# Splitting the inputs of four projections in quarters, each next to the weight pieces that need it

## The chip, the cores and the metric

The kernel runs on one core of a Trainium2 chip. The metric is device time in microseconds (us) for one execution, median of several. A core has TensorE (PE: matmuls, and PEld: its weight loads), VectorE (DVE), ScalarE (ACT), GpSimd (POOL), and queues of DMA transfers, most of them issued by SyncE (SP). Each engine works through its own program in order and waits on semaphores that others raise.

## The reference

Two transformer blocks over 256 tokens with 2048 features, in float32. Cut to what matters:

```python
# first block
u = rmsnorm(h, mix_norm_w)
p = u @ w_in                          # columns for DeltaNet, then for RWKV
h = h + concat([o_dn, o_rw]) @ w_out  # mixer output
h = h + memory_cross_attention(...)
h = h + square(relu(rmsnorm(h, ffn_norm_w) @ w1)) @ w2   # MLP, 2048 -> 8192 -> 2048
x = rmsnorm(h, final_norm_w)
# second block; c is one vector
mod = silu(c) @ w_mod + b_mod + mod_layer      # six vectors: shift, scale, gate
h = rms_norm(x, norm1_g) * (1 + scale1) + shift1
proj = h @ w_in_2                     # second mixer, 2560 columns
x = x + gate1 * (y @ w_out_2)
x = x + gate2 * hierarchical_moe(...) # 32 experts, 2 per token
```

## The kernel before

The stages follow each other in blocks (`nc.Block`): at a block's end all engines meet, and at its start each takes up its next program. On the way from one to the next some 0.3 us pass.

**Split products.** The large matmuls keep float32 accuracy with TensorE's fast format (`fp32r`): a matrix a is split into a high part, which is a copy in that format made by ScalarE, and a low part, a minus its high part, made by VectorE. The product is then three matmuls: high x high, low x high and high x low. Both factors are split, the weights piece by piece as TensorE goes, and the input once at the start of the stage. The input is 128 x 16 chunks x 256 tokens, that is 4096 elements per partition.

The change touches four stages that do so:

- `rwkv_project` (class `SplitTiles`, methods L284 to L325). 24 output tiles; each is one product over 16 chunks, in two halves of 8 chunks. A weight piece is a half tile, 128x1024, with one buffer per half. TensorE spends 24 matmuls of 256 columns on a half. The first piece of the product reads only chunks 0 to 7 of the input.
- `mixer_out` (class `SplitRows`, L350 to L395): output 256 x 2048 in 4 groups of 512 columns. A group is 8 pieces of 2 chunks each, 128x1024, in 4 buffers; TensorE spends 12 matmuls of 512 columns on one. Piece p reads chunks 2p and 2p+1 of the input.
- `mlp` (L2067, class `Ffn`): 16 blocks of 512 hidden features. `order` lists the pieces (128x2048, 3 high and 3 low buffers, 4 raw ones that DMA fills): four up pieces of block 0, then in turn four up pieces of a block and four down pieces of the one before. An up piece covers 4 chunks of the input and takes 48 matmuls of 256 columns. VectorE also sums the modulation here (`sum_after`, L603): from piece 4 on, 96 multiply-adds over 128x2048, whose weights arrive in `mod_raw` beside the MLP's.
- `second_mixer` (L2242 on): `SplitRows` with 5 groups.

**Order at a stage's start.** In the first, second and fourth of these ScalarE makes the whole high part in two halves (`input_high`), then the high parts of weight pieces; VectorE makes both low halves (`input_low`), then low parts of pieces. TensorE waits for the low part of its first piece. In `mlp` each engine makes the input's part in one instruction, in a block of its own, ScalarE also calculates silu(c) there, and the pieces start in the next block. The buffer `shared`, which holds the MLP's input u, is the one in which the modulation is summed: GpSimd clears it (`mod.clear`, L597), SP then loads the bias into it (`loads_with`, with weight load 6), and VectorE adds from there. `deltanet_project` uses `SplitTiles` too and keeps its order.

Of the kernel before, what the change touches and what calls it, by code (L numbers as in the profile page):

```python
# [10 lines left out]
F32 = mybir.dt.float32  # L11
# [252 lines left out]
class SplitTiles:  # L264
# [62 lines left out]
class SplitRows:  # L327
# [22 lines left out]
    def input_high(self, act, x):  # L350
        for n in range(2):
            act.activation(self.x_hi[:, 8 * n:8 * n + 8], x[:, 8 * n:8 * n + 8, :], ACT.Copy).then_inc(self.k.act_sem, 1)

    def input_low(self, dve, x):
        for n in range(2):
            dve.wait_ge(self.k.act_sem, self.k.act_n + n + 1)
            dve.tensor_tensor(self.x_lo[:, 8 * n:8 * n + 8], x[:, 8 * n:8 * n + 8, :],
                              self.x_hi[:, 8 * n:8 * n + 8].bitcast(F32), ALU.subtract)
# [448 lines left out]
def deltanet_project(nc, k, tiles, qkvz, dn):  # L807
# [3 lines left out]
    with nc.Block(no_gpsimd_drain=True) as block:  # L811
# [324 lines left out]
def rwkv_project(nc, k, tiles, u, mix):  # L1136
# [5 lines left out]
    with nc.Block(no_gpsimd_drain=True) as block:  # L1142
# [24 lines left out]
        @block.scalar  # L1167
        def _(act):
            tiles.input_high(act, u)
            with act.Fori(0, 3) as i:  # L1170
                for m in range(8):
                    tiles.high(act, m, (0, 1), turn=i)

        @block.vector
        def _(dve):
            s.eng = dve

            tiles.input_low(dve, u)
# [8 lines left out]
            tiles.low(dve, 0, (0, 1))  # L1187
# [22 lines left out]
    k.act_n += 2  # L1210
# [2250 lines left out]
```

## Time and profile before

| what | us |
|---|---|
| median of 3 runs | 2546.53 |
| lowest, highest | 2545.34, 2548.73 |
| the profiled execution | 2547.53 |
| its span, first to last instruction | 2545.9 |
| busy in it: TensorE, VectorE, ScalarE | 2268.4, 1335.5, 789.8 |
| mean granted TensorE clock, share of full speed | 0.922 |

All times in the rows are from the start of the span of that one execution. A row of the timeline has the start, the duration, engine, source line, and what is written from what; a row with xN stands for N instructions of a kind in a row, with the time from the start of the first to the end of the last. In square brackets is how long the engine had been idle, and who released it. The names are the kernel's tensors: `rw_u_hi` and `rw_w_lo` are the input's high and the weight's low part in RWKV, `out_` in the mixer output, `in_` in the second mixer, `u_` and `ffn_w_` in the MLP.

### The profile page before, as it was taken

Reading aid. Unit: us, or ns where it says so; the run is one execution under the profiler, and the core shown is the slowest. Engines: PE = TensorE matmul, PEld = TensorE weight load, DVE = VectorE, ACT = ScalarE, POOL = GpSimd, SP = SyncE. Lnnn points to the kernel's source line nnn. Section 1 sums busy time; section 2 is a strip of 40 time slices with the busy share of each in tenths; the row PEclk is TensorE's granted clock in tenths of the full one; section 3 lists DMA queues with packets and bytes.
Section 4 is the critical chain, followed back from the end, with each engine's and each line's share of the span. In section 5 each row is a group of like instructions: output and inputs, shape, how many; then the busy total and the mean of one; then the engine's idle time right before and its main releaser. Section 6 shows DMA issues by size and latency. Waiting matters only on the chain. (4 is left out here: it accounts for less than half of the span.)

```text
span 2545.9 us, 40044 instructions
## 1 busy us (share of the span) xinstructions
PE 2268.4 (89%) x17032; PEld 1829.4 (72%) x17032; DVE 1335.5 (52%) x1604; ACT 789.8 (31%) x917; POOL 18.6 (1%) x62
## 2 busy tenths in 40 slices
PE   7998799878889987999999999997979787888884
PEld 7998799677867657899999899985854443444441
DVE  4776655565453125888787988865552411111112
ACT  4444333311243024434343434335430211111110
POOL 0000000000000000000000000000000000000000
PEclk8999899877889998999999999998989788889987
DMA  5453035100044316888798888845420599999998
GB/s 207 180 198 133 2 132 198 58 2 1 2 184 179 133 59 250 334 332 321 283 356 321 323 323 325 341 152 205 187 98 33 233 419 426 427 423 427 422 428 330
DMA packets 67288, 597.51 MB, mean 235 GB/s; under 512 B 9518, under 2 KB 9774, under 8 KB 16686
## 3 DMA queue, kind: packets, MB, share of 16 engines
q1 hardware_dynamic: 56906, 572.15, 56.2%
q10 hardware_dynamic: 9216, 12.60, 1.4%
q0 software_dynamic: 1008, 10.49, 1.0%
q8 instruction: 121, 1.98, 0.3%
q14 instruction: 37, 0.30, 0.0%
HBM read 674.88 MB, written 14.68 MB: 271 GB/s over the span
## 5 line engine op out<-in xcount | busy, mean ns | idle before, releaser
L2052 ACT ACTIVATE ffn_w_hi<-ffn_raw 128x2048 fp32r<-128x2048 f32 x128 | 245.0, 1916 | 372.0 <-PE psum L2097 368.7
L2059 DVE TENSOR_TENSOR ffn_w_lo<-ffn_raw,ffn_w_hi 128x2048 fp32r<-128x2048 f32 x128 | 292.6, 2289 | 90.7 <-ACT ffn_w_hi L2052 90.7
L2095 PE MATMUL psum<-u_hi,ffn_w_hi 128*128 128x256 f32 x1024 | 293.9, 287 | 15.0 <-DVE ffn_w_lo L2059 13.9
L2096 PE MATMUL psum<-u_lo,ffn_w_hi 128*128 128x256 f32 x1024 | 293.3, 286 | 0.0
L2097 PE MATMUL psum<-u_hi,ffn_w_lo 128*128 128x256 f32 x1024 | 293.3, 286 | 0.0
L2921 PE MATMUL psum<-moe_raw,moe_x_t 128*32 128x512 f32 x1536 | 217.8, 700 | 70.5 <-DMA moe_raw<-in_moe 62.9
L614 DVE SCALAR_TENSOR_TENSOR shared<-mod_raw,c_silu,shared 128x2048 f32<-128x2048 f32 x96 | 225.3, 2347 | 0.0
L2095 PEld LDWEIGHTS psum<-u_hi,ffn_w_hi 128*128 128x128 f32 x1024 | 200.2, 196 | 15.8 <-DVE ffn_w_lo L2059 14.1
L2096 PEld LDWEIGHTS psum<-u_lo,ffn_w_hi 128*128 128x128 f32 x1024 | 200.0, 195 | 0.4
L2097 PEld LDWEIGHTS psum<-u_hi,ffn_w_lo 128*128 128x128 f32 x1024 | 200.1, 195 | 0.0
L2096 PE MATMUL psum<-ffn_w_lo,ffn_hid_hi 128*128 128x512 f32 x512 | 199.4, 389 | 0.0
L2095 PE MATMUL psum<-ffn_w_hi,ffn_hid_hi 128*128 128x512 f32 x512 | 199.4, 389 | 0.0
L2097 PE MATMUL psum<-ffn_w_hi,ffn_hid_lo 128*128 128x512 f32 x512 | 199.3, 389 | 0.0
L2921 PEld LDWEIGHTS psum<-moe_raw,moe_x_t 128*32 128x32 f32 x1536 | 49.2, 120 | 179.1 <-issue 151.0
L321 PE MATMUL psum<-dn_u_hi,dn_w_hi 128*128 128x256 f32 x512 | 146.4, 286 | 0.0
L323 PE MATMUL psum<-dn_u_hi,dn_w_lo 128*128 128x256 f32 x512 | 145.6, 284 | 0.0
L322 PE MATMUL psum<-dn_u_lo,dn_w_hi 128*128 128x256 f32 x512 | 145.6, 284 | 0.0
L3066 DVE TENSOR_TENSOR moe_hid<-moe_silu,psum 128x64 f32<-128x64 f32 x48 | 10.6, 221 | 212.8 <-ACT moe_silu L2997 212.8
L321 PE MATMUL psum<-rw_u_hi,rw_w_hi 128*128 128x256 f32 x384 | 110.0, 287 | 9.7 <-DVE rw_w_lo L310 9.7
L2911 PEld LDWEIGHTS psum<-moe_place,xn_hi 128*128 128x128 f32 x384 | 77.4, 202 | 50.1 <-issue 47.6
L2097 PEld LDWEIGHTS psum<-ffn_w_hi,ffn_hid_lo 128*128 128x128 f32 x512 | 96.1, 188 | 20.2
L2095 PEld LDWEIGHTS psum<-ffn_w_hi,ffn_hid_hi 128*128 128x128 f32 x512 | 96.2, 188 | 20.1
(605 smaller groups left out, 4339.7 us busy)
## 6 DMA issues: line engine op xcount, KB each, us to landing
moe_raw<-in_moe SPq DMA_DIRECT2D x96, 2048.0 KB, 16.8
ffn_raw<-in_ffn SPq DMA_DIRECT2D x128, 1024.0 KB, 5.2
ring<-in_stream SPq DMA_DIRECT2D x59, 2048.0 KB, 12.1
mod_raw<-in_mod SPq DMA_DIRECT2D x96, 1024.0 KB, 7.4
moe_raw<-in_moe POOLq DMA_DIRECT2D x48, 2048.0 KB
expert_rows<-moe_stage ACTq DMA_DIRECT2D x192, 64.0 KB, 8.6
x<-in_x SPq DMA_DIRECT2D x2, 1024.0 KB, 5.9
u<-in_mem SPq DMA_DIRECT2D x2, 1024.0 KB, 15.6
```

The source lines that it names most:

```text
L321: pe.matmul(out, hi, self.u_hi[:, chunk, :], start=chunk == 0, stop=False)
L322: pe.matmul(out, hi, self.u_lo[:, chunk, :], start=False, stop=False)
L323: mm = pe.matmul(out, lo, self.u_hi[:, chunk, :], start=False, stop=chunk == KC - 1)
L614: dve.scalar_tensor_tensor(at, self.raw[:, i % self.RAWS], self.c_silu[:, c:c + 1], at, ALU.mult, ALU.add)\
L2052: act.activation(self.w_hi[:, number % self.HIGHS], self.raw[:, number % self.RAWS], ACT.Copy)\
L2059: dve.tensor_tensor(self.w_lo[:, number % self.LOWS], self.raw[:, number % self.RAWS], self.w_hi[:, number % self.HIGHS].bitcast(F32), ALU ...
L2095: pe.matmul(out, lhs[0], rhs[0], start=start, stop=False)
L2096: pe.matmul(out, lhs[0], rhs[1], start=False, stop=False)
L2097: return pe.matmul(out, lhs[1], rhs[0], start=False, stop=stop)
L2911: pe.matmul(gathers(piece)[:, c, :], xn_hi[:, t, own], rows, start=t == 0, stop=False)
L2921: mm = pe.matmul(summed(tile)[strip(q), :], e.x_t[:, tile // 4 % 2, UNIT_KC * u + c, strip(tile % 4)], w[:, c * COLS:(c + 1) * COLS], star ...
L3066: dve.tensor_tensor(e.hid[:, tile % 2], e.silu[:, tile % 2], folds(tile)[:, 1], ALU.mult).then_inc(e.hid_done, 1)
```

## The change

The input is split in quarters of 4 chunks, and the instructions of a quarter stand between those for the first weight pieces. `input_high` and `input_low` now do one part of the input instead of all.

- RWKV: two quarters, first half piece, two quarters, second half piece, on both engines. Two small VectorE instructions (`one_less_mu`, `one_less_ka`) move behind that. ScalarE's loop over the tiles starts with tile 1, runs 2 turns of 8, and the last 7 tiles are written out.
- Mixer output and second mixer: `first_high` and `first_low`. ScalarE: quarter, pieces 0 and 1, quarter, pieces 2 and 3, two quarters, pieces 4 to 7. VectorE: each quarter directly before its two pieces. In the mixer output the loops over groups are written out, TensorE's too.
- MLP: the block for the input is gone. In the one block each of the first four pieces comes after its quarter; silu(c) follows the fourth quarter. GpSimd's clearing waits until the fourth low part is made (`f.low` at 4), since the input is read until then.
- `deltanet_project` calls the new methods with the old halves; its order is the same.

The diff, without repeats of the same edit in `SplitRows.input_*` and in `deltanet_project`:

```diff
-    def input_high(self, act, u):
-        for n in range(2):
-            act.activation(self.u_hi[:, 8 * n:8 * n + 8], u[:, 8 * n:8 * n + 8, :], ACT.Copy).then_inc(self.k.act_sem, 1)
-
-    def input_low(self, dve, u):
-        for n in range(2):
-            dve.wait_ge(self.k.act_sem, self.k.act_n + n + 1)
-            dve.tensor_tensor(self.u_lo[:, 8 * n:8 * n + 8], u[:, 8 * n:8 * n + 8, :],
-                              self.u_hi[:, 8 * n:8 * n + 8].bitcast(F32), ALU.subtract)
+    def input_high(self, act, u, n, chunks=8):
+        own = slice(chunks * n, chunks * n + chunks)
+        act.activation(self.u_hi[:, own], u[:, own, :], ACT.Copy).then_inc(self.k.act_sem, 1)
+
+    def input_low(self, dve, u, n, chunks=8):
+        own = slice(chunks * n, chunks * n + chunks)
+        dve.wait_ge(self.k.act_sem, self.k.act_n + n + 1)
+        dve.tensor_tensor(self.u_lo[:, own], u[:, own, :], self.u_hi[:, own].bitcast(F32), ALU.subtract)
...
+    def input_low(self, dve, x, n):
+        dve.wait_ge(self.k.act_sem, self.k.act_n + n + 1)
+        dve.tensor_tensor(self.x_lo[:, 4 * n:4 * n + 4], x[:, 4 * n:4 * n + 4, :],
+                          self.x_hi[:, 4 * n:4 * n + 4].bitcast(F32), ALU.subtract)
+
+    def first_high(self, act, x):
+
+        for n in range(4):
+            self.input_high(act, x, n)
+            if n < 2:
+                self.high(act, 0, (2 * n, 2 * n + 1))
+        self.high(act, 0, range(4, 8))
+
+    def first_low(self, dve, x, half):
+
+        for n in (2 * half, 2 * half + 1):
+            self.input_low(dve, x, n)
+            self.low(dve, 0, (2 * n, 2 * n + 1))
...
         @block.scalar
         def _(act):
-            tiles.input_high(act, u)
-            with act.Fori(0, 3) as i:
-                for m in range(8):
+            for half in range(2):
+                for n in (2 * half, 2 * half + 1):
+                    tiles.input_high(act, u, n, 4)
+                tiles.high(act, 0, (half,))
+            with act.Fori(0, 2) as i:
+                for m in range(1, 9):
                     tiles.high(act, m, (0, 1), turn=i)
+            for m in range(17, 24):
+                tiles.high(act, m, (0, 1))
 
         @block.vector
         def _(dve):
             s.eng = dve
 
-            tiles.input_low(dve, u)
+            for half in range(2):
+                for n in (2 * half, 2 * half + 1):
+                    tiles.input_low(dve, u, n, 4)
+                tiles.low(dve, 0, (half,))
...
@@ -1184,7 +1205,6 @@
                 s.step(dve.tensor_scalar(now, ps[:, 0:T], less, None, ALU.mult))
                 s.settle()
                 dve.scalar_tensor_tensor(later, ps[:, 0:T - 1], mu, later, ALU.mult, ALU.add).then_inc(k.ft_free, 1)
-            tiles.low(dve, 0, (0, 1))
...
         @block.tensor
         def _(pe):
-            with pe.Fori(0, 2) as i:
-                for g in range(2):
-                    rows.group(pe, g, turn=i)
+            for g in range(4):
+                rows.group(pe, g)
 
         @block.scalar
         def _(act):
-            rows.input_high(act, mixed)
-            with act.Fori(0, 2) as i:
-                for g in range(2):
-                    rows.high(act, g, range(8), turn=i)
+            rows.first_high(act, mixed)
+            for g in range(1, 4):
+                rows.high(act, g, range(8))
...
-            rows.input_low(dve, mixed)
-            for g in range(4):
+            for half in range(2):
+                rows.first_low(dve, mixed, half)
+            for g in range(1, 4):
                 rows.low(dve, g, range(4))
-                if g:
-                    add(g - 1)
+                add(g - 1)
                 rows.low(dve, g, range(4, 8))
             add(3)
...
 def mlp(nc, k, f, mod, x, u, u_hi, u_lo):
-    with nc.Block(no_gpsimd_drain=True) as block:
-        @block.scalar
-        def _(act):
-            act.activation(u_hi[:], u[:], ACT.Copy).then_inc(k.act_sem, 1)
-            act.activation(mod.c_silu[:], cols_of(k, "c"), ACT.Silu)
-
-        @block.vector
-        def _(dve):
-            dve.wait_ge(k.act_sem, k.act_n + 1)
-            dve.tensor_tensor(u_lo[:], u[:], u_hi[:].bitcast(F32), ALU.subtract)
-    k.act_n += 1
+    QUARTERS = 4
+
+    def quarter(a, n):
+        return a[:, 4 * n:4 * n + 4, :]
     order = f.order()
...
-        block.gpsimd(mod.clear)
+        @block.gpsimd
+        def _(pool):
+            pool.wait_ge(f.low, QUARTERS)
+            mod.clear(pool)
...
             for number in range(len(order)):
+                if number < QUARTERS:
+                    act.activation(quarter(u_hi, number), quarter(u, number), ACT.Copy).then_inc(k.act_sem, 1)
+                if number == QUARTERS - 1:
+                    act.activation(mod.c_silu[:], cols_of(k, "c"), ACT.Silu).then_inc(k.act_sem, 1)
...
             for number in range(len(order)):
+                if number < QUARTERS:
+                    dve.wait_ge(k.act_sem, k.act_n + number + 1)
+                    dve.tensor_tensor(quarter(u_lo, number), quarter(u, number), quarter(u_hi, number).bitcast(F32),
+                                      ALU.subtract)
+                if number == QUARTERS:
+                    dve.wait_ge(k.act_sem, k.act_n + QUARTERS + 1)
...
-            rows.input_low(dve, h_t)
-            for g in range(5):
+            for half in range(2):
+                rows.first_low(dve, h_t, half)
+            for g in range(1, 5):
                 rows.low(dve, g, range(4))
...
-            rows.input_high(act, h_t)
-            for g in range(5):
+            rows.first_high(act, h_t)
+            for g in range(1, 5):
                 rows.high(act, g, range(4))
-                if g:
-                    take(g - 1)
+                take(g - 1)
                 rows.high(act, g, range(4, 8))
```

What stands on VectorE at the start of the RWKV projection, before:

```order
L1174 UNCONDITIONAL_BRANCH [waits barrier_Pool_Activation_PE_DVE_SP_release]
L291 TENSOR_TENSOR rw_u_lo<-u,rw_u_hi 128x2048 [waits act_sem] x2
L1179 TENSOR_SCALAR one_less_mu<-cols 128x26
L1180 TENSOR_SCALAR one_less_ka<-cols 128x8
L310 TENSOR_TENSOR rw_w_lo<-ring,rw_w_hi 128x1024 [waits piece_high,dve_sem]
L310 TENSOR_TENSOR rw_w_lo<-ring,rw_w_hi 128x1024 [waits piece_high]
L1188 UNCONDITIONAL_BRANCH
```

and now:

```order
L1192 UNCONDITIONAL_BRANCH [waits barrier_Pool_Activation_PE_DVE_SP_release]
L291 TENSOR_TENSOR rw_u_lo<-u,rw_u_hi 128x1024 [waits act_sem] x2
L309 TENSOR_TENSOR rw_w_lo<-ring,rw_w_hi 128x1024 [waits piece_high]
L291 TENSOR_TENSOR rw_u_lo<-u,rw_u_hi 128x1024 [waits act_sem] x2
L309 TENSOR_TENSOR rw_w_lo<-ring,rw_w_hi 128x1024 [waits piece_high]
L1200 TENSOR_SCALAR one_less_mu<-cols 128x26
L1201 TENSOR_SCALAR one_less_ka<-cols 128x8
L1208 UNCONDITIONAL_BRANCH [waits dve_sem]
```

L291 is the input's low part, L310 (L309 now) a weight piece's. The first weight piece moved up past half of the input and past the two small instructions; the second stands behind the other half.

ScalarE from the end of the norm to the MLP's fourth piece, before:

```order
L174 UNCONDITIONAL_BRANCH
L2069 UNCONDITIONAL_BRANCH [waits barrier_Pool_Activation_PE_DVE_SP_release]
L2071 ACTIVATE u_hi<-shared 128x4096
L2072 ACT_TABLE_LOAD
L2072 ACTIVATE c_silu<-cols 128x16
L2068 UNCONDITIONAL_BRANCH
L2138 UNCONDITIONAL_BRANCH [waits barrier_Pool_Activation_PE_DVE_SP_release]
L2052 ACTIVATE ffn_w_hi<-ffn_raw 128x2048 [waits ffn_raw_in0]
L2052 ACTIVATE ffn_w_hi<-ffn_raw 128x2048 [waits ffn_raw_in1]
L2052 ACTIVATE ffn_w_hi<-ffn_raw 128x2048 [waits ffn_raw_in2]
L2052 ACTIVATE ffn_w_hi<-ffn_raw 128x2048 [waits ffn_used,ffn_raw_in3]
```

and now:

```order
L174 UNCONDITIONAL_BRANCH
L2152 UNCONDITIONAL_BRANCH [waits barrier_Pool_Activation_PE_DVE_SP_release]
L2165 ACTIVATE u_hi<-shared 128x1024
L2070 ACTIVATE ffn_w_hi<-ffn_raw 128x2048 [waits ffn_raw_in0]
L2165 ACTIVATE u_hi<-shared 128x1024
L2070 ACTIVATE ffn_w_hi<-ffn_raw 128x2048 [waits ffn_raw_in1]
L2165 ACTIVATE u_hi<-shared 128x1024
L2070 ACTIVATE ffn_w_hi<-ffn_raw 128x2048 [waits ffn_raw_in2]
L2165 ACTIVATE u_hi<-shared 128x1024
L2167 ACT_TABLE_LOAD
L2167 ACTIVATE c_silu<-cols 128x16
L2070 ACTIVATE ffn_w_hi<-ffn_raw 128x2048 [waits ffn_used,ffn_raw_in3]
```

L2071 (L2165 now) writes the input's high part, L2052 (L2070) a weight piece's. One branch pair, the block between input and weights, is gone, the input comes in four instructions, and the table load for silu stands behind the third piece.

## Rows read from the trace of the kernel before

**Rows 1.** The page's busy shares: busy us (share of the span) xinstructions.
```profile
PE 2268.4 (89%) x17032; PEld 1829.4 (72%) x17032; DVE 1335.5 (52%) x1604; ACT 789.8 (31%) x917; POOL 18.6 (1%) x62
```

**Rows 2.** TensorE's waits, whole span: line waited for, us in total, times, longest.
```profile
PE psum L2921 <- DMA moe_raw<-in_moe: 62.9, 25, 6.6
...
PE psum L392 <- DVE in_w_lo L377: 13.6, 1, 13.6
```

**Rows 3.** Timeline, RWKV projection: start, duration, engine, line, [idle before <-releaser].
```profile
304.14 3.71 ACT L286 ACTIVATE rw_u_hi<-u 128x2048 fp32r<-128x2048 f32 x2 [4.96 <-PEq L1002]
306.08 4.49 DVE L291 TENSOR_TENSOR rw_u_lo<-u,rw_u_hi 128x2048 fp32r<-128x2048 f32 x2 [2.50 <-ACT rw_u_hi L286]
...
310.77 2.36 DVE L310 TENSOR_TENSOR rw_w_lo<-ring,rw_w_hi 128x1024 fp32r<-128x1024 f32 x2
...
312.05 0.58 PE L321 MATMUL psum<-rw_u_hi,rw_w_hi 128*128 128x256 f32 x1 [9.69 <-DVE rw_w_lo L310]
...
317.56 0.41 PE L322 MATMUL psum<-rw_u_lo,rw_w_hi 128*128 128x256 f32 x1
...
317.58 1.06 ACT L304 ACTIVATE rw_w_hi<-ring 128x1024 fp32r<-128x1024 f32 x1 [7.84 <-PE psum L323]
317.77 0.36 PE L323 MATMUL psum<-rw_u_hi,rw_w_lo 128*128 128x256 f32 x1
...
317.96 0.28 PE L321 MATMUL psum<-rw_u_hi,rw_w_hi 128*128 128x256 f32 x1
...
318.08 0.28 PE L322 MATMUL psum<-rw_u_lo,rw_w_hi 128*128 128x256 f32 x1
...
318.67 1.23 DVE L310 TENSOR_TENSOR rw_w_lo<-ring,rw_w_hi 128x1024 fp32r<-128x1024 f32 x1 [5.54 <-ACT rw_w_hi L304]
```

**Rows 4.** Timeline, mixer output.
```profile
705.56 3.71 ACT L352 ACTIVATE out_x_hi<-mixed 128x2048 fp32r<-128x2048 f32 x2 [8.07 <-PEq L3292]
...
709.18 3.88 ACT L371 ACTIVATE out_w_hi<-ring 128x1024 fp32r<-128x1024 f32 x4
711.92 4.62 DVE L377 TENSOR_TENSOR out_w_lo<-ring,out_w_hi 128x1024 fp32r<-128x1024 f32 x4
...
713.19 0.79 PE L392 MATMUL psum<-out_w_hi,out_x_hi 128*128 128x512 f32 x1 [12.67 <-DVE out_w_lo L377]
...
717.20 0.44 PE L392 MATMUL psum<-out_w_hi,out_x_hi 128*128 128x512 f32 x1
```

**Rows 5.** Timeline, start of the MLP.
```profile
957.83 3.62 ACT L2071 ACTIVATE u_hi<-shared 128x4096 fp32r<-128x4096 f32 x1 [0.33 <-PEq L174]
...
966.23 3.55 POOL L601 MEMSET shared<- 128x2048 f32 x2 [965.64 <-POOLq L2068]
...
970.54 0.58 PE L2095 MATMUL psum<-u_hi,ffn_w_hi 128*128 128x256 f32 x1 [13.92 <-DVE ffn_w_lo L2059]
...
976.47 0.38 PE L2095 MATMUL psum<-u_hi,ffn_w_hi 128*128 128x256 f32 x1
```

**Rows 6.** Timeline of VectorE, MLP, the fourth weight piece.
```profile
981.30 2.29 DVE L2059 TENSOR_TENSOR ffn_w_lo<-ffn_raw,ffn_w_hi 128x2048 fp32r<-128x2048 f32 x1 [6.41 <-ACT ffn_w_hi L2052]
```

**Rows 7.** Timeline, start of the second mixer.
```profile
1738.95 3.71 ACT L352 ACTIVATE in_x_hi<-h_t 128x2048 fp32r<-128x2048 f32 x2 [0.33 <-PEq L174]
...
1746.67 0.76 PE L392 MATMUL psum<-in_w_hi,in_x_hi 128*128 128x512 f32 x1 [13.59 <-DVE in_w_lo L377]
```

**Rows 8.** Two windows of the MLP: length, busy per engine, PEclk, DMA share, GB/s.
```profile
960.00:964.00 4.00, 0.00 (x0) 0.00 (x0) 2.52 (x1) 2.94 (x3) 0.00 (x0) 0.50 0.00 0
1064.00:1109.00 45.00, 45.00 (x292) 41.24 (x292) 37.66 (x24) 18.40 (x11) 0.00 (x0) 1.00 0.89 339
```

**Rows 9.** DMA issues 1724.5 to 1725, then 975.2 to 975.4: last number us to landing.
```profile
ring<-in_stream SPq DMA_DIRECT2D x1, 2048.0 KB, 8.4
...
ffn_raw<-in_ffn SPq DMA_DIRECT2D x1, 1024.0 KB, 10.1
```

**Rows 10.** The page's instruction groups: xcount | busy, mean ns | idle before, releaser.
```profile
L2052 ACT ACTIVATE ffn_w_hi<-ffn_raw 128x2048 fp32r<-128x2048 f32 x128 | 245.0, 1916 | 372.0 <-PE psum L2097 368.7
```

More of the change, by code:

```diff
@@ L348, in weights, with input_high @@
         return self.k.ring[:, unit % SLOTS, row:row + 2, :].rearrange("p c n -> p (c n)")
[L350 to L358, printed above, removed]
+    def input_high(self, act, x, n):
+        act.activation(self.x_hi[:, 4 * n:4 * n + 4], x[:, 4 * n:4 * n + 4, :], ACT.Copy).then_inc(self.k.act_sem, 1)
+    def input_low(self, dve, x, n):
[12 more added lines that the diff above has]
+            self.low(dve, 0, (2 * n, 2 * n + 1))
     def high(self, act, g, pieces, turn=None):
@@ L834, in _ @@
             s.eng = dve
-            tiles.input_low(dve, dn.u)
+            for n in range(2):
+                tiles.input_low(dve, dn.u, n)
             tiles.low(dve, 0, (0, 1))
@@ L870, in _ @@
             d0 = k.dve_at
-            tiles.input_high(act, dn.u)
+            for n in range(2):
+                tiles.input_high(act, dn.u, n)
             tiles.high(act, 0, (0, 1))
@@ L1209, in _ @@
                       mix[:, 24 + m, 1:T])
-    k.act_n += 2
+    k.act_n += 4
     k.ft += 26
@@ L1588, in add @@
                     dve.tensor_tensor(at, at, bank(k, 4 + (t0 + 2 * g + t) % 4), ALU.add).then_inc(k.tt_free, 1)
-            rows.input_low(dve, mixed)
-            for g in range(4):
+            for half in range(2):
+                rows.first_low(dve, mixed, half)
+            for g in range(1, 4):
                 rows.low(dve, g, range(4))
-                if g:
-                    add(g - 1)
+                add(g - 1)
                 rows.low(dve, g, range(4, 8))
             add(3)
-    k.act_n += 2
+    k.act_n += 4
     rows.end(4)
@@ L2181, in _ @@
                 gather(e, j - f.HALVES)
+    k.act_n += QUARTERS + 1
 def final_norm(nc, k, io, x, weight, squares, gates, mod_cols, scale1, scale2):
@@ L2301, in _ @@
             take(4)
-    k.act_n += 2
+    k.act_n += 4
     rows.end(5)
```

## The prediction

> **What bounds the kernel now.** I read the busy shares first, then the waits of TensorE over the whole span, then the timeline around each long wait. TensorE is busy for 89% of the span [rows 1], so a microsecond is won where TensorE stands still and something after it moves up. Of its waits the longest in total, 62.9 us in 25 pieces, is for expert weights near the end [rows 2] and isn't touched. Four of the next ones are single waits, each at the start of one of the projections that the change edits: 13.9 us (MLP), 13.6 (second mixer), 12.7 (mixer output) and 9.7 (RWKV) [rows 3, 4, 5, 7]. Each ends on VectorE's first low part of a weight piece. Their sum, 49.9 us, is the ceiling, but most of it is work that stays.
>
> The timelines show what stands in them. In RWKV ScalarE starts at 304.14 with two halves of the input's high part, VectorE follows with two low halves from 306.08 to 310.57, then two small scalings (order above, `one_less_mu` and `one_less_ka`), and only at 310.77 does it come to the weight piece that TensorE's first matmul (312.05) needs [rows 3]. The mixer output has the same form from 705.56 to 713.19 [rows 4]. The MLP does its input in one instruction per engine, in a block of its own: ScalarE from 957.83 for 3.62 us, then VectorE; GpSimd's first instruction behind the block change comes at 966.23, and only then the first piece of weights is split; TensorE starts at 970.54 [rows 5]. The second mixer goes from 1738.95 to 1746.67 [rows 7]. So each start is a serial chain ScalarE, VectorE, TensorE, and VectorE's whole input stands in it although the first matmuls need a quarter or a half of it.
>
> **The change, part by part.** RWKV at full length. The instructions have known prices, since a quarter of the input has the shape of a weight piece (128x1024): 1.06 us alone on ScalarE and 1.23 us alone on VectorE [rows 3]. In a row they follow each other every (3.88 - 1.06) / 3 = 0.94 us and (4.62 - 1.23) / 3 = 1.13 us [rows 4]. Now VectorE may start at 304.14 + 1.06 + 0.04 (ScalarE's first half ends at 304.14 + 1.90 = 306.04, VectorE starts at 306.08) = 305.24; the second quarter follows at 306.37, the weight piece at 307.50 (its high part is out at 304.14 + 2 x 0.94 + 1.06 = 307.08), it ends at 308.73, and TensorE starts 0.05 us later, at 308.78. Gain: 312.05 - 308.78 = 3.27 us. What is late next is the second half: two more quarters and a piece on VectorE, out at 308.63 + 2 x 1.13 + 1.23 = 312.12. TensorE needs it after 24 matmuls, which start 0.21 us apart at the slow clock (317.56, 317.77), at 313.9. The two small scalings come behind it, at 312.3, and are first wanted when the first product is complete. Cover 1.8 us, cost nothing; without it the price would be those 3.4 us.
>
> Mixer output. VectorE needs one quarter and one weight piece ahead of TensorE: 705.56 + 1.06 + 0.04 = 706.66, piece at 707.79 (high part out at 707.56), done at 709.02, TensorE at 709.07. Gain 713.19 - 709.07 = 4.12 us. The next piece is out 1.13 us later, while TensorE spends 12 matmuls of twice the width on one, 12 x 0.42 = 5.1 us at the slow clock. Quarter 2 reaches VectorE behind piece 3, by 714.8, and is first read by piece 4; that piece needs a buffer that piece 0 leaves at 714.2, as before. Quarter 3 stands on VectorE in front of piece 6, 1.1 us against the 12 x 2 x 0.12 = 2.9 us that TensorE takes per piece at the full clock. TensorE's loop becomes straight code, which no row of this stage shows. The second mixer already is straight code and has one wait, its first [rows 2]; so 0 at one end. At the other a wait as long as a block change, 0.33 us [rows 7], and as much below nothing, since the loop's own turn goes. I take 0.
>
> Second mixer. The same edit, with start at 1738.95: VectorE 1740.05, piece 1741.18, done 1742.41, TensorE 1742.5. Gain 1746.67 - 1742.5 = 4.2 us. The high part of piece 0 is now read from the ring at 1739.9. Its load is issued between 1724.5 and 1725 and lands 8.4 us later [rows 9], near 1733, so it is there.
>
> MLP. The block change goes, and so does the order input before weights. ScalarE from 957.83: quarter 0 to 958.89, piece 0 from 958.77 to 960.68. VectorE: quarter 0 from 958.93, piece 0 from 960.72 to 963.01 (a piece of 128x2048 takes 2.29 us [rows 6]); TensorE at 963.05. Gain 970.54 - 963.05 = 7.5 us. Quarter 1 and piece 1 follow on VectorE to 966.4, quarter 2 and piece 2 to 969.6, quarter 3 to 970.7. TensorE takes 48 matmuls per piece: 48 x 0.12 = 5.8 us at the full clock, and for the first, with 5.9 us at the slow one (28 matmuls), 5.9 + 20 x 0.12 + 0.3 = 8.6 us. It wants piece 1 at 971.7, 5 us after it is there. Silu and its table load follow quarter 3 on ScalarE, to 968.6, before piece 3 can start (971.7).
> One wait is added. GpSimd's two memsets (3.55 us [rows 5]) overwrote the input's buffer once it was free; they now wait for low part 3, out at 971.7 + 1.9 + 2.3 = 975.9. The bias load on SP's queue waits for the first memset, to 977.7; behind it stands weight load 7, else due at 975.9. That is 1.8 us late. The weight load next to the bias took 10.1 us to land [rows 9], and this piece is wanted when piece 4 is used up, at 971.7 + 4 x 5.8 = 994.9. VectorE waits for the bias before its first modulation sum, which stands behind low part 4, and all later low parts stand behind the sum. Piece 1 is used up at 977.5, low part 4 is done at 981.7, so the sum is due 4 us after the bias is issued. Low part 5 is wanted at 994.9, so TensorE feels it only if the sum starts after 994.9 - 2.3 - 2.3 = 990.3. I put the chain at 0; its upper end is that of rival (d).
>
> Does the gain last? In the MLP TensorE is the engine waited for: ScalarE was idle 372 us before its weight pieces, 368.7 of it for TensorE [rows 10]. In a typical 45 us of it TensorE is busy throughout, VectorE 37.7 us, the DMA engines 0.89 of the time [rows 8]: near, but not the bound. Later loads are issued on semaphores that the same engines raise, so they move along. The expert stage is bound by its loads [rows 2], whose first are issued by the router's block, and that moves too.
> Sum: 3.3 + 4.1 + 7.5 + 4.2 = 19.1 us. The profiled execution took 2547.5 (span 2545.9), 1.0 above the median of 2546.5. So 2528.5 against itself, 2527.5 against the median; I say **2528**.
>
> **The clock.** The stages start at half clock (1.2 GHz): matmuls are 0.21 us apart, later 0.12 at 2.4 GHz [rows 3]. The slow stretch lasts 5.8, 4.0 and 6.0 us where its end is shown (312.05 to 317.8, 713.19 to 717.2, 970.54 to 976.5) [rows 3, 4, 5]. A slow microsecond costs 1 - 0.12 / 0.21 = 0.43 us, so four stretches of a mean 5.3 us cost 9. Nothing in the edit fixes where the stretch ends; if each new one lies anywhere from 4.0 to 6.0, the sum moves by up to 3 us either way, and I keep that for the range.
> The Trainium skill, TensorE: Matmul & The Clock Gate (Part 1: The HAM clock gate), says that the gate works to a beat which is "free-running — it doesn't reset when your kernel starts". By that rule each slow stretch is drawn anew and the sum is 19 with some scatter; by the rows taken as they stand each stage keeps its own and it is 19.1 sharp. The three unequal stretches speak for the rule.
>
> **Rivals.** (a) The shorter gap leaves the clock up. The gap shrinks to 6.5 us in RWKV and 6.4 in the MLP. Then all slow stretches go and another 9 us with them: 2519. Against it: the clock is at 0.50 all through 960 to 964 [rows 8], in which the MLP's new start (963.05) falls, and that gap is the one that shrinks most. The Trainium skill, TensorE: Matmul & The Clock Gate (Why this matters for your kernels), advises short idle gaps so that the clock is kept; read so it backs this rival, and no run here shows it yet.
> (b) The MLP's head start is taken back: loads at 0.89 of the DMA engines hold the pace, and its 7.5 us go. Then 3.3 + 4.1 + 4.2 = 11.6, and 2535. For it speaks the DMA share, against it that ScalarE, which reads the loads first, waits for TensorE in 368.7 of 372 us [rows 10].
> (c) All of it is taken back further on, by a stage whose loads don't start earlier (the experts'): 2546, no change. Against it: those loads are issued behind the router.
> (d) Slower: the bias chain in the MLP. GpSimd, then SP, then the bias, then VectorE's first sum, behind which stand all later low parts. TensorE is touched if the bias lands after 990.3, 12.6 us after its issue. To use up the whole 19.1 us it must land 31.7 us after it; at 40 us the time is 2547.5 + 8.3 = 2556. The load next to it landed in 10.1 us [rows 9].
> That the change might not do what it says is excluded by the order of the instructions, which shows the quarters between the pieces.
>
> **Chances.** Forecast 0.85, its own range 2523 to 2533 (3 for the clock, 2 for the runs of before, which are 3.4 us apart). (a) 0.03, (b) 0.06, (c) 0.03, (d) 0.03. A measurement tells no change from a change within some 0.2%, 5 us. Faster: 0.85 + 0.03 + 0.06 = 0.94, less 0.01 for what is unnamed; same 0.04; slower 0.03. The range: 2522 to 2534 leaves out (a), (c), (d), a part of (b), and edges.
>
> **What would show it.** TensorE's four waits at 6.4, 8.6, 6.4 and 9.4 us, and no new wait for a low part within the first ten pieces; the first sum of the modulation within 20 us of the MLP's first matmul; GpSimd's memsets some 13 us after that matmul; the same length from the MLP's start to the end of the span as now (2545.9 - 970.5 = 1575.4), give or take 3. A wait of ScalarE for ffn_raw would speak for (b), a wait of VectorE's first sum for (d), matmuls of 0.12 us spacing right at a start for (a). I am wrong if TensorE starts each stage earlier and the span doesn't follow.

## The result

The changed kernel takes 2528.07 us (median of 4 runs, 2520.88 to 2530.3), the kernel before 2547.38 (4 runs, 2545.34 to 2548.73): ratio 0.992, 95% interval 0.9902 to 0.9939, so 0.6 to 1.0% faster. The forecast was 2528, range 2522 to 2534. Two later groups of runs on other occasions gave 0.9928 (0.9914 to 0.9941) and 0.9933 (0.992 to 0.9946).

| us | before | after |
|---|---|---|
| span of the profiled execution | 2545.9 | 2528.6 |
| TensorE's wait: RWKV, mixer output, MLP, second mixer | 9.7, 12.7, 13.9, 13.6 | 6.4, 8.7, 6.4, 9.5 |
| granted clock, mean | 0.922 | 0.925 |

The page of after, its busy shares and ScalarE's pieces of the MLP, answering to [rows 1] and [rows 10]:

```profile
PE 2269.4 (90%) x17032; PEld 1831.8 (72%) x17032; DVE 1336.2 (53%) x1613; ACT 790.4 (31%) x926; POOL 18.6 (1%) x62
...
L2070 ACT ACTIVATE ffn_w_hi<-ffn_raw 128x2048 fp32r<-128x2048 f32 x128 | 245.2, 1916 | 364.6 <-PE psum L2111 364.6
...
L2109 PE MATMUL psum<-u_hi,ffn_w_hi 128*128 128x256 f32 x1024 | 294.3, 287 | 7.6 <-DVE ffn_w_lo L2077 6.4
```

TensorE is as busy as before (2269.4 against 2268.4 us) in a shorter span. All of ScalarE's idle time before its pieces, 364.6 us, ends on TensorE. The third row is the first of the three matmuls of each up product (high x high): TensorE was idle 7.6 us in front of it in the whole MLP, 6.4 of it the wait at the start.

The timeline of after at the start of RWKV, answering to [rows 3]:

```profile
305.25 2.00 ACT L286 ACTIVATE rw_u_hi<-u 128x1024 fp32r<-128x1024 f32 x2 [4.97 <-PEq L1015]
306.34 2.36 DVE L291 TENSOR_TENSOR rw_u_lo<-u,rw_u_hi 128x1024 fp32r<-128x1024 f32 x2 [1.65 <-ACT rw_u_hi L286]
307.16 1.04 ACT L303 ACTIVATE rw_w_hi<-ring 128x1024 fp32r<-128x1024 f32 x1
308.11 1.99 ACT L286 ACTIVATE rw_u_hi<-u 128x1024 fp32r<-128x1024 f32 x2
308.62 1.22 DVE L309 TENSOR_TENSOR rw_w_lo<-ring,rw_w_hi 128x1024 fp32r<-128x1024 f32 x1
309.75 2.35 DVE L291 TENSOR_TENSOR rw_u_lo<-u,rw_u_hi 128x1024 fp32r<-128x1024 f32 x2
...
309.89 0.58 PE L320 MATMUL psum<-rw_u_hi,rw_w_hi 128*128 128x256 f32 x1 [6.42 <-DVE rw_w_lo L309]
...
312.02 1.22 DVE L309 TENSOR_TENSOR rw_w_lo<-ring,rw_w_hi 128x1024 fp32r<-128x1024 f32 x1
...
313.16 0.17 DVE L1200 TENSOR_SCALAR one_less_mu<-cols 128x26 f32<-128x26 f32 x1
...
315.17 0.41 PE L320 MATMUL psum<-rw_u_hi,rw_w_hi 128*128 128x256 f32 x1
```

Two quarters on VectorE (306.34), one weight piece (308.62), and TensorE starts at 309.89, 4.6 us after ScalarE; before it was 7.9. The other two quarters (309.75) and the second piece, out at 313.24, run while TensorE is in its first 24 matmuls. The 25th, the first to read them, starts at 315.17 without a wait. Slack 1.8 us was forecast, 1.9 is there.

The start of the MLP in after, answering to [rows 5]:

```profile
951.98 1.06 ACT L2165 ACTIVATE u_hi<-shared 128x1024 fp32r<-128x1024 f32 x1 [0.33 <-PEq L174]
952.95 1.89 ACT L2070 ACTIVATE ffn_w_hi<-ffn_raw 128x2048 fp32r<-128x2048 f32 x1
953.07 1.23 DVE L2191 TENSOR_TENSOR u_lo<-shared,u_hi 128x1024 fp32r<-128x1024 f32 x1 [2.90 <-ACT u_hi L2165]
...
954.87 2.29 DVE L2077 TENSOR_TENSOR ffn_w_lo<-ffn_raw,ffn_w_hi 128x2048 fp32r<-128x2048 f32 x1 [0.57 <-ACT ffn_w_hi L2070]
...
957.08 1.22 DVE L2191 TENSOR_TENSOR u_lo<-shared,u_hi 128x1024 fp32r<-128x1024 f32 x1
957.19 7.00 SPq L2052 DMA_DIRECT2D ffn_raw<-in_ffn  x3
...
957.22 0.58 PE L2109 MATMUL psum<-u_hi,ffn_w_hi 128*128 128x256 f32 x1 [6.45 <-DVE ffn_w_lo L2077]
...
961.30 1.28 ACT L2167 ACT_TABLE_LOAD   x1
```

ScalarE begins at 951.98, and TensorE 5.2 us later (12.7 before). Quarters (1.06, 1.23 us) and pieces (1.89, 2.29 us) alternate on both engines. The table load for silu (961.30) comes when ScalarE is through with the first three pieces.

### The profile page after: what moved, and what is told of

It is laid out like the page before. It is cut to its first block and busy times, and to the rows that moved or that the text cites. A ratio compares the mean times of both kernels' runs of the same rounds, so it can differ in the third digit from the quotient of the medians.

```text
span 2528.6 us, 39996 instructions
## 1 busy us (share of the span) xinstructions
PE 2269.4 (90%) x17032; PEld 1831.8 (72%) x17032; DVE 1336.2 (53%) x1613; ACT 790.4 (31%) x926; POOL 18.6 (1%) x62
## 5 line engine op out<-in xcount | busy, mean ns | idle before, releaser
L2070 ACT ACTIVATE ffn_w_hi<-ffn_raw 128x2048 fp32r<-128x2048 f32 x128 | 245.2, 1916 | 364.6 <-PE psum L2111 364.6
L3097 DVE TENSOR_TENSOR moe_stage<-psum,gate_rows 128x512 f32<-128x512 f32 x48 | 33.2, 692 | 150.8 <-PE psum L2969 150.8
```

What stands on the lines that cost most here:

```text
L2070: act.activation(self.w_hi[:, number % self.HIGHS], self.raw[:, number % self.RAWS], ACT.Copy)\
```

## Experiments

The table cuts each profiled execution at ScalarE's first instruction on the input in the four stages. "Chain" is the time from there to TensorE's first matmul on it. "Slow" is how long after that matmul the 0.21 us spacing (twice that for 512 columns) lasts. Both are read from the timelines ("slow" to about 0.1 us), and the lengths add up to the span.

| run | to RWKV | to mixer output | to MLP | to second mixer | to the end | chain | slow |
|---|---|---|---|---|---|---|---|
| before | 304.1 | 401.4 | 252.3 | 781.1 | 807.0 | 7.9, 7.6, 12.7, 7.7 | 5.9, 4.0, 6.0, 4.8 |
| after | 305.2 | 397.8 | 248.9 | 774.1 | 802.6 | 4.6, 3.6, 5.2, 3.6 | 5.9, 5.1, 3.6, 6.1 |
| mlp_only | 305.2 | 401.4 | 252.3 | 770.8 | 805.9 | 7.9, 7.6, 5.2, 7.7 | 5.9, 4.0, 3.4, 4.8 |
| others_only | 305.1 | 397.8 | 247.9 | 781.6 | 799.0 | 4.6, 3.6, 12.7, 3.6 | 5.9, 5.1, 4.0, 3.0 |
| after_again | 308.8 | 396.3 | 248.2 | 771.4 | 799.7 | 4.6, 3.6, 5.2, 3.6 | 4.9, 5.7, 5.1, 3.1 |
| after_third | 307.4 | 397.6 | 248.8 | 774.1 | 802.3 | 4.6, 3.6, 5.2, 3.6 | 5.5, 4.8, 3.5, 6.1 |
| mlp_in_row | 306.0 | 398.3 | 248.9 | 777.1 | 799.4 | 4.6, 3.6, 8.1, 3.6 | 3.0, 5.1, 4.2, 3.1 |
| bias_late4 | 305.0 | 397.8 | 248.9 | 771.0 | 804.9 | 4.6, 3.6, 5.2, 3.6 | 5.8, 5.1, 3.6, 5.7 |
| bias_late8 | 308.0 | 397.7 | 248.9 | 777.2 | 798.7 | 4.6, 3.6, 5.2, 3.6 | 5.7, 4.8, 3.6, 3.0 |
| warm | 306.0 | 398.2 | 247.5 | 772.5 | 798.5 | 5.8, 5.4, 5.2, 5.7 | 0.3, 0.4, 0.3, 0.5 |
| warm2 | 305.0 | 394.7 | 247.4 | 771.0 | 803.6 | 4.6, 3.6, 5.2, 3.6 | 0.2, 1.0, 0.2, 0 |
| early2 | 307.5 | 397.6 | 247.6 | 767.5 | 800.0 | 4.6, 3.6, 3.5, 3.6 | 0.2, 1.4, 0.2, 0.4 |
| early2_again | 304.9 | 397.7 | 247.7 | 767.8 | 800.0 | 4.6, 3.6, 3.5, 3.6 | 0.3, 1.8, 0.3, 0 |

**mlp_only and others_only: does each part bring its own?** The MLP's functions of after in the kernel before, and those of before in the changed kernel. Expected:

> The kernel before with the changed MLP alone. Serial-chain theory: the MLP's first wait of TensorE falls from 13.9 to 6.4 us, the three other waits stay at 9.7, 12.7 and 13.6, and the time is 7.5 us below the kernel before (2540 against 2547.4), +-3 for where TensorE's slow stretches end. Rival (taken back in the MLP, by loads or VectorE): the wait falls as well but the length from the MLP's first matmul to the end grows by about as much, and the time stays at 2547.

> The changed kernel with the MLP of before; RWKV, mixer output and second mixer keep the change. Serial-chain theory: waits of TensorE 6.4, 8.7 and 9.5 us in those three and 13.9 in the MLP, time 3.3 + 4.1 + 4.2 = 11.6 us below the kernel before, about 2536. With the kernel that has the MLP alone the two gains add up to the whole one, 19. Rival (one stage's gain hides in another's): the two don't add up.

Measured beside a median of before of 2545.38 (9 runs): 2537.32 for the MLP alone, 8.1 less (ratio 0.9965, 0.9951 to 0.9978), and 2535.93 for the other three, 9.5 less (the same ratio and interval). Together 17.5, against 19.3 of the whole change in the same group (after_again, next). The waits came out as expected and the chains repeat to 0.1 us in the table. Each stage's length falls where its own edit is and stays where it isn't: 401.4 and 252.3 with mlp_only, 781.6 with others_only. By how much it falls in one profile is less exact: the MLP is 10.3 us shorter in mlp_only (its chain 7.5), the last stretch 8.0 in others_only (its chain 4.1); the clock, next, accounts for the MLP's. The rival of mlp_only falls. The two gains add up as far as the runs can tell, and nothing speaks for the rival of others_only.

**after_again and after_third: how much do runs of one kernel differ?**

> The changed kernel once more, for the spread between its runs: 2520.9 to 2530.3 in four. Theory (slow stretches of TensorE's clock fall differently in each execution): median 2528 +-2, again with several us between runs, and a span of the profiled run that differs from 2528.6 by about 0.43 us for each us of slow clock under work. Rival (the low run was a single accident): all within 3 us.

> The changed kernel beside early2: 19 us below the kernel before (the forecast's sum), +-2, and 6 to 8 above early2.

Measured: 2526.08 (2525.95 to 2529.85, 5 runs) and 2528.98 (2525.4 to 2531.96, 6 runs), 19.3 and 16.0 below the kernel before of their groups (2545.38 and 2544.97). Both medians lie in the 2526 to 2530 that was expected, but 16.0 misses the 19 +-2 expected of after_third. The low run of 2520.88 did not come again in 11. The chains are the same to 0.1 us, so what varies is elsewhere. The slow stretches behind the four starts, 20.7, 18.8 and 19.9 us together, explain too little: after_again's profile is 4.2 us shorter than after's, where 1.9 us at 0.43 give 0.8.

TensorE also works at the slow clock elsewhere. In the stretch ahead of RWKV, whose order of work the change leaves as it was, the windows (length, busy us and instructions of PE, PEld, DVE, ACT, POOL, granted clock, DMA share, GB/s) of after and of after_again read

```profile
220.00:240.00 20.00, 17.84 (x102) 14.61 (x100) 13.31 (x32) 7.26 (x15) 0.00 (x0) 1.00 0.53 211
```

```profile
220.00:240.00 20.00, 17.84 (x86) 14.37 (x86) 10.39 (x24) 4.66 (x7) 0.00 (x0) 0.83 0.54 211
```

TensorE is busy for 17.84 us in both and gets less done in the second. 0.83 over 20 us is 6.8 us at the lower level, 2.9 us at 0.43, and RWKV starts 3.6 us later in that profile (308.8 against 305.2). The same can be summed for a whole stage: in each window of 1 us, TensorE's busy time times the share of the window at the lower level, (1 - clock) x 2. For the MLP:

| run | MLP | chain | later wait | slow and busy | what is left at 0.43 |
|---|---|---|---|---|---|
| before | 781.1 | 12.7 | 0 | 22.7 | 758.6 |
| after | 774.1 | 5.2 | 0 | 24.0 | 758.6 |
| mlp_only | 770.8 | 5.2 | 0 | 16.6 | 758.5 |
| others_only | 781.6 | 12.7 | 0 | 24.4 | 758.4 |
| after_again | 771.4 | 5.2 | 0 | 18.5 | 758.2 |
| after_third | 774.1 | 5.2 | 0 | 24.0 | 758.6 |
| mlp_in_row | 777.1 | 8.1 | 0 | 24.7 | 758.4 |
| bias_late4 | 771.0 | 5.2 | 0 | 16.8 | 758.6 |
| bias_late8 | 777.2 | 5.2 | 3.5 | 23.0 | 758.6 |
| early2_again | 767.8 | 3.5 | 0 | 13.3 | 758.6 |

The last column is the length less the chain, less the later wait and less 0.43 times the slow us. It is the same to 0.4 us in lengths that are up to 13.8 us apart. So in the MLP the chain counts in full, a slow us costs 0.43, and little else varies. Ahead of RWKV the clock goes with most of the difference (slow and busy 21.7 us in before, 31.5 in bias_late8, in windows of 2 us; lengths 304.1 and 308.0); for the last stretch it isn't shown.

**mlp_in_row: order or missing block?**

```diff
-                if number < QUARTERS:
-                    act.activation(quarter(u_hi, number), ...)
+                if number == 0:
+                    for n in range(QUARTERS):
+                        act.activation(quarter(u_hi, n), ...)
```

and the same for the low quarters on VectorE.

> The changed kernel with the MLP's four quarters in a row ahead of the first weight piece on both engines: one block, quarters, but nothing between them. Theory: VectorE does four quarters (to about 5.7 us after ScalarE's start), then the piece, and TensorE starts 8.0 us after it; changed kernel 5.2, kernel before 12.7. So of the MLP's 7.5 us, 4.7 come from the missing block change and from ScalarE and VectorE working on different quarters, and 2.8 from the order. Rival (the order brings all of it): close to 12.

Measured: one run, 2531.35; the chain is 8.1 us, 8.0 was expected. So of the MLP's 7.5 us, 4.6 (12.7 - 8.1) are from one block in place of two and quarters that let VectorE begin early, and 2.9 (8.1 - 5.2) from putting pieces between them. The stage is 777.1 us long against 771.4 to 774.1 in the changed kernel; less what the slow clock takes, it is the chain's 2.9 (table above). The rival falls. How the 4.6 divide between the block and the quarters isn't shown.

**bias_late8 and bias_late4: where rival (d) would begin.**

```diff
             pool.wait_ge(f.low, QUARTERS)
+            for n in range(8):                  # 4 in bias_late4
+                pool.memset(mod.sums[:, 0, :], 0.0).then_inc(f.delayed, 1)
+                pool.wait_ge(f.delayed, n + 1)
             mod.clear(pool)
```

> The changed kernel with eight more memsets on GpSimd ahead of the clearing, so that the modulation's bias is loaded some 14 us later, at 28 us after the MLP's first matmul in place of 14. It computes the same. Theory of the prediction (slack of about 12 us from the bias's issue, then TensorE waits): the first sum starts near 30 us after the first matmul, low part 5 follows, and TensorE, which wants it at 30.7, waits 4 to 7 us there, once; the span grows by that. Rival (VectorE's backlog or the queued loads cost more, as rival (d) has it): several waits and more than 10 us. Second rival (slack is larger): no wait.

> Four more memsets in place of eight: the bias is issued some 7.5 us later than in the changed kernel, about 21.5 us after the MLP's first matmul, and lands 2.1 us later as with eight. The first sum then starts at 23.7, low part 5 is out at 28.3, and TensorE wants it at 30.7. Theory (slack 12 us): TensorE has no second wait, and the MLP takes as long as in the changed kernel. Rival (VectorE's backlog costs TensorE time even within the slack): a wait in the following block, or the MLP longer by over 2 us.

The timelines and waits of bias_late8:

```profile
971.71 14.87 POOL L2106 MEMSET shared<- 128x2048 f32 x8 [971.12 <-DVE ffn_w_lo L2078]
986.63 3.55 POOL L612 MEMSET shared<- 128x2048 f32 x2
```

```profile
988.47 0.32 SPq L606 DMA_DIRECT2D shared<-in_mod_bias  x1
```

```profile
990.57 2.35 DVE L625 SCALAR_TENSOR_TENSOR shared<-mod_raw,c_silu,shared 128x2048 f32<-128x2048 f32 x1 [13.10 <-DMA shared<-in_mod_bias]
992.84 2.28 DVE L2078 TENSOR_TENSOR ffn_w_lo<-ffn_raw,ffn_w_hi 128x2048 fp32r<-128x2048 f32 x1
```

```profile
PE psum L2113 <- DVE ffn_w_lo L2078: 9.9, 2, 6.4
```

```profile
995.17 0.58 PE L2113 MATMUL psum<-u_hi,ffn_w_hi 128*128 128x256 f32 x1 [3.47 <-DVE ffn_w_lo L2078]
...
1000.68 0.39 PE L2114 MATMUL psum<-u_lo,ffn_w_hi 128*128 128x256 f32 x1
1000.89 0.29 PE L2115 MATMUL psum<-u_hi,ffn_w_lo 128*128 128x256 f32 x1
```

```profile
992.00:994.00 2.00, 0.00 (x0) 0.00 (x0) 2.00 (x2) 0.30 (x1) 0.00 (x0) 1.00 1.07 451
...
996.00:998.00 2.00, 2.00 (x11) 2.00 (x11) 2.00 (x2) 0.00 (x0) 0.00 (x0) 0.50 0.82 262
```

The bias is issued 28.8 us after the first matmul (959.7), VectorE's first sum follows 2.1 us later after a wait of 13.1, and TensorE has a second wait, 9.9 - 6.4 = 3.5 us. That wait also loses the clock: it was at 1.00 before, it is at 0.50 after, and the matmuls from 995.17 to 1000.89 are 0.21 us apart again. So the late bias costs 3.5 us and another slow stretch of 5.7 us at 0.43, 2.5: 6.0 together. The MLP is 777.2 us long (time of the one run: 2532.11). With four memsets the same row of VectorE reads:

```profile
980.20 2.35 DVE L625 SCALAR_TENSOR_TENSOR shared<-mod_raw,c_silu,shared 128x2048 f32<-128x2048 f32 x1 [5.54 <-DMA shared<-in_mod_bias]
```

```profile
PE psum L2113 <- DVE ffn_w_lo L2078: 6.4, 1, 6.4
```

Its sum starts 23.3 us after the first matmul (956.9), VectorE has waited 5.5 us, and TensorE only has its wait at the start; the MLP takes 771.0, no longer than in the changed kernel, and 6.2 less than with eight (time 2529.29). So the chain is real. TensorE would have wanted low part 5 at 991.70, 3.47 us before it came, so the latest sum that costs nothing is one at 30.9 - 3.5 = 27.4 us; the prediction's 990.3 is 27.3 after its 963.05. Behind that TensorE waits once, 3.5 us where 4 to 7 were expected; the slow stretch after the wait, which nobody had reckoned with, brings it to 6.0. The changed kernel's own sum is at 17.7. VectorE makes the backlog good. The rivals of both runs fall.

**warm: what the slow start costs.** In front of TensorE's program in each stage:

```diff
+def warm(k, pe, b, count):
+    for n in range(count):
+        pe.matmul(bank(k, b)[:, 0:T], const(k, "ones"), k.consts[:, 0:T], start=True, stop=True)
```

> The changed kernel with matmuls of no use (ones by a constant, 128x256, into a bank that nobody reads then) in front of TensorE's first wait in the four stages: 9 in RWKV, 7 in each mixer stage, 11 in the MLP, meant to end before the wait does. Theory (the slow stretch after each start is paid in full, 0.43 us a us, and ends a while after TensorE has become busy, whatever it computes): the real matmuls start at the same place but their slow stretch shrinks from 4 to 6 us to 0 to 3, so 4 x 4 x 0.43 = about 7 us less than the changed kernel, 2521. Rival (the clock doesn't answer to such matmuls, or they overrun the wait): the stretches stay as long and the time stays at 2528 or rises by what they overrun.

RWKV in warm, TensorE's timeline:

```profile
306.04 6.08 PE L419 MATMUL psum<-consts 128*128 128x256 f32 x18 [1.80 <-PEq L1020]
311.78 0.47 PE L320 MATMUL psum<-rw_u_hi,rw_w_hi 128*128 128x256 f32 x1
312.08 0.28 PE L321 MATMUL psum<-rw_u_lo,rw_w_hi 128*128 128x256 f32 x1
312.20 0.28 PE L322 MATMUL psum<-rw_u_hi,rw_w_lo 128*128 128x256 f32 x1
```

Measured: 2524.42 us (2515.78 to 2525.76), 1.7 below after_again in the same group. The means of the five runs, 2521.5 and 2527.3, are 5.8 apart, so these runs don't tell 2 us from the 7 that were expected. The traces say more. The clock answers: the real matmuls stand 0.12 us apart (0.23 for 512 columns) from their second on, in all four stages. But in three stages they start late, since 9 matmuls are 18 instructions and take 5.7 us, so the chain grew to 5.8, 5.4 and 5.7 us: 1.2 + 1.8 + 2.1 = 5.1 us lost. In the MLP the clock was at 1.00 and eleven took 4.99 us, in time. Against the loss the slow stretches are 17.3 us shorter than in after_again, 7.4 at 0.43; the difference is 2.3. Both theories were half right.

**warm2: fewer of them** (5, 4, 6, 4).

> The kernel of the run warm with fewer useless matmuls, since each was two instructions and took about 0.8 us at the slow clock: there they held the real ones up by 1.1, 1.8 and 2.1 us in RWKV, mixer output and second mixer. Now 5, 4, 6 and 4. Theory (a slow stretch costs 0.43 us a us, an overrun 1 us a us): the real matmuls start where they do in the changed kernel (4.6, 3.6, 5.2, 3.6 us after ScalarE's first quarter), their slow stretches are 0 to 3 us in place of 3 to 6, and the time is about 6 us below the changed kernel: 2520 against 2526. Rival (the clock's stretches are made up elsewhere): 2524 to 2526.

The chains are back at 4.6, 3.6, 5.2 and 3.6, the slow stretches are at most 1.0. Time 2523.32 (2517.45 to 2526.21) beside before at 2547.41: 24.1 below (0.9904, 0.9886 to 0.9921), where the changed kernel was 19.3 below in the groups until then. So 4.8 of the 6 that were expected. The two stood in different groups, though, after_third's later group gave 16.0, and the intervals of warm2 and of after_again (0.9914 to 0.9941) overlap: the chains and slow stretches are shown, the size of the gain only roughly.

**early2: the MLP's first piece out of the chain.** On top of warm2 the MLP's buffers are opened ahead of the norm, in which ScalarE then makes the first piece's high part, and VectorE starts the MLP with the low one:

```diff
                .then_inc(k.norm_rms, 1)
+            if beside is not None:
+                beside(act)                   # f.split_high(act, 0), in the MLP's norm
...
+            f.split_low(dve, 0)               # then quarter 0, and TensorE waits for that
```

> warm2, and the MLP's first weight piece taken out of the chain: its high part is made in the norm's block, where ScalarE is idle for 3.7 us, and its low part while VectorE would wait for the first quarter. Theory (the chain is the sum of what stands in it): TensorE's first MLP matmul comes 3.5 us after ScalarE's first quarter in place of 5.2, 1.7 us less than warm2 and about 2518. Rival (the high part holds up the norm on ScalarE, or its load isn't there): the norm gets longer by up to 1.9 us and nothing is won.

> early2 once more, beside the changed kernel on one chip, since the two stood in different groups of runs. Theory (four slow stretches of 3 to 6 us at 0.43, and 1.7 us from the MLP's first piece): 6 to 8 us below the changed kernel. Rival (the earlier difference came from the chip): within 2 us of it.

The start in early2_again, timelines of ScalarE, VectorE and TensorE:

```profile
943.73 1.91 ACT L2080 ACTIVATE ffn_w_hi<-ffn_raw 128x2048 fp32r<-128x2048 f32 x1 [0.73 <-DMA ffn_raw<-in_ffn]
...
950.33 2.00 ACT L2177 ACTIVATE u_hi<-shared 128x1024 fp32r<-128x1024 f32 x2 [0.32 <-PEq L174]
```

```profile
950.36 2.29 DVE L2087 TENSOR_TENSOR ffn_w_lo<-ffn_raw,ffn_w_hi 128x2048 fp32r<-128x2048 f32 x1 [0.86 <-PEq L174]
952.57 2.35 DVE L2205 TENSOR_TENSOR u_lo<-shared,u_hi 128x1024 fp32r<-128x1024 f32 x2
```

```profile
950.36 1.96 PE L421 MATMUL psum<-consts 128*128 128x256 f32 x8 [1.77 <-PEq L174]
953.84 0.39 PE L2119 MATMUL psum<-u_hi,ffn_w_hi 128*128 128x256 f32 x1 [1.52 <-DVE u_lo L2205]
```

The piece's high part (L2080) is made inside the norm. At the MLP's start only its low part (950.36) and quarter 0 (952.57) are left, and TensorE begins at 953.84, 3.5 us after ScalarE's 950.33. Four useless matmuls took 1.96 us and left a wait of 1.5.

Chain 3.5 us in both profiles, as expected, and the stage is 767.5 and 767.8 us long against 771.0 in warm2. The norm did not get longer (247.6 and 247.7 us from mixer output to MLP, 247.4 in warm2), so that rival falls. The step from warm2 alone, 1.4 us by the medians, is within what runs differ by. Times: 2521.89 (2517.71 to 2525.09) at 2547.41 for before, and 2521.03 (2513.43 to 2527.56) at 2544.97, ratios 0.9899 (0.9884 to 0.9913) and 0.9906 (0.9887 to 0.9924). Beside the changed kernel in one group it is 8.0 us lower (2528.98), the upper end of what was expected. It has the lowest median of all versions; against after the intervals of the two ratios, 0.9887 to 0.9924 and 0.992 to 0.9946, overlap by a hair.

## Why the prediction was right

- **The ceiling and the chains.** The sum of known durations held to 0.1 us: TensorE's starts were forecast 4.6, 3.5, 5.2 and 3.6 us after ScalarE's, and are 4.6, 3.6, 5.2 and 3.6. The four waits were forecast at 6.4, 8.6, 6.4 and 9.4 and are 6.4, 8.7, 6.4 and 9.5. It worked since the shape of a quarter already stood in the trace as a weight piece's. That the median came out at 2528 to 0.1 us is luck: three groups of runs gave 19.3, 19.3 and 16.0 below the kernel before, for 19.1 in the sum.
- **The covers.** RWKV's second half and the MLP's later pieces are never waited for; straight code in the mixer output costs nothing that shows (one wait of TensorE there).
- **The bias chain at 0.** Forecast: memsets 12.9 us after the first matmul, bias at 14.7, sum at 18.7. Measured 12.0, 13.9 and 17.7, early because the slow stretch was 3.6 us and not 5.9. What was argued of its slack, the runs with delayed clearing show: 27.4 us after the first matmul where the prediction's numbers give 27.3.
- **Does it last.** Yes: the table's stage lengths fall by 3.6, 3.4, 7.0 and 4.4 us, 18.4 in all. The span fell by 17.3, since this execution was 1.1 us later at RWKV's start.
- **Two slips.** The length from the MLP's first matmul to the end was to stay at 1575.4. It is 2528.6 - 957.2 = 1571.4. The second mixer's own 4.2 us lie within it and had not been taken off; the sum did have them. And weight load 7 brings piece 7, counted from 0, which is wanted when piece 6 is used up and not piece 4, some 12 us later than written; the cover was larger than claimed and the cost stays 0.
- **The clock.** The stretches did change by stage: 5.9, 5.1, 3.6 and 6.1 us, 20.7 together, as before in sum, and one stage's differs between runs of one kernel (the second mixer's 6.1, 3.1, 6.1). By that the rule of the Trainium skill, TensorE: Matmul & The Clock Gate (Part 1: The HAM clock gate), of a free-running beat agrees with the runs. The bound of 4.0 to 6.0 for each was too narrow, 3.0 to 6.1 over the kernels without warming. It also looked at the four starts alone, while the clock is low elsewhere too: the MLP has 16.6 to 24.7 us of it under work in the kernels without warming, 3.4 to 6.0 of them at its start. That a slow us costs 0.43 holds in the MLP (table above).
- **The rivals.** (a) did not happen: the gap of 6.4 us in the MLP was still followed by a slow stretch. Windows of after around it (fine, then coarse), and of warm below, in the columns given above:

```profile
950.40:950.60 0.20, 0.20 (x2) 0.09 (x1) 0.00 (x0) 0.00 (x0) 0.00 (x0) 0.50 0.00 0
950.60:950.80 0.20, 0.17 (x1) 0.00 (x0) 0.00 (x0) 0.00 (x0) 0.00 (x0) 0.92 0.10 41
```

```profile
948.00:950.00 2.00, 2.00 (x12) 2.00 (x11) 2.00 (x6) 1.09 (x3) 0.00 (x0) 0.50 0.81 332
950.00:952.00 2.00, 0.78 (x4) 0.49 (x3) 0.17 (x1) 0.86 (x3) 0.00 (x0) 0.84 0.04 16
952.00:954.00 2.00, 0.00 (x0) 0.00 (x0) 0.93 (x1) 2.00 (x2) 0.00 (x0) 1.00 0.46 86
954.00:956.00 2.00, 0.00 (x0) 0.00 (x0) 1.43 (x2) 2.00 (x3) 0.00 (x0) 0.51 1.06 446
956.00:958.00 2.00, 0.78 (x3) 0.78 (x4) 2.00 (x2) 2.00 (x2) 0.00 (x0) 0.50 0.97 401
```

```profile
948.00:950.00 2.00, 2.00 (x17) 1.88 (x16) 2.00 (x6) 1.62 (x4) 0.00 (x0) 0.92 0.99 418
950.00:952.00 2.00, 0.26 (x2) 0.22 (x2) 0.96 (x3) 1.21 (x4) 0.00 (x0) 1.00 0.23 94
952.00:954.00 2.00, 2.00 (x10) 1.77 (x10) 1.12 (x1) 2.00 (x2) 0.00 (x0) 1.00 0.55 115
954.00:956.00 2.00, 2.00 (x11) 1.74 (x11) 1.43 (x2) 2.00 (x3) 0.00 (x0) 1.00 1.02 430
```

In after the norm's matmuls run at 0.50; the clock comes up in the last 0.2 us of their work (950.6), stays at 1.00 while TensorE has nothing to do, and is down again (0.51, then 0.50) before the first real matmul comes at 957.22. In warm TensorE idled 1.74 us, went on with useless matmuls at 951.81, and the clock stayed at 1.00. The advice of the Trainium skill, TensorE: Matmul & The Clock Gate (Why this matters for your kernels), to keep idle gaps short agrees with that. The prediction took it as speaking for (a); but a gap cut to 6.4 us was not short enough here, nor was the one of 3.5 us in bias_late8. (b) and (c): with ScalarE waiting for TensorE in 364.6 of 364.6 us, and stages that all keep their gain, neither has a place left. (d) exists and begins 27.4 - 17.7 = 9.7 us later than where the changed kernel stands.

Open: why TensorE's clock is low in one execution and not in another at the same place of the program (220 to 240 us above), and what makes the last stretch 798.7 to 804.9 us long over kernels that are alike in it.

## What to carry to other kernels

At the start of a stage, write down what the first matmul really reads, and put just that, from every engine, in front of it; the rest hides behind the first pieces. Sum it from rows with the same shape and check what each moved clearing or load now waits for, with the slack in us. A gap that has to stay can be filled with matmuls of no use, but count their instructions: a us of overrun costs a full us, a us of slow clock 0.43. And before comparing one stage of two profiles, take out what the slow clock cost in each.

## What was not expected of the hardware

The granted clock can come up just as TensorE runs out of work and be lost before its next matmul, so that neither gains by it: 0.50 until 950.6, 1.00 with TensorE idle from 950.8, 0.51 from 954 on in the MLP's gap above. A single wait of 3.5 us in the middle of the MLP cost 2.5 us more by the slow stretch behind it (bias_late8). A float32 matmul of 128 by 256 columns is two instructions: eleven took 4.99 us at clock 1.00 in the MLP of warm, 0.45 us each, against 0.12 for an fp32r one of that width. A small load (16 KB) was used 2.1 us after its issue (bias_late8). And the same kernel, before, ran from 2539.34 to 2552.16 us over all groups, so a change of 5 us needs more than a few runs.
